# Adding the gates of three heads into a cleared DRAM map with indirect accumulating DMAs from GpSimd

## What is computed

```python
def peer_ffn(h, w_query, q_norm_peer, sub_keys_1, sub_keys_2, expert_u, expert_v):
    qr = rms_norm((h @ w_query).reshape(bsz, seq, PEER_HEADS, PEER_DKEY), q_norm_peer)
    ...
    v1, i1 = lax.top_k(s1, PEER_TOPK)
    v2, i2 = lax.top_k(s2, PEER_TOPK)
    ...
    top_s, top_pos = lax.top_k(cand_s, PEER_TOPK)
    idx = jnp.take_along_axis(cand_i, top_pos, axis=-1)
    g = jax.nn.softmax(top_s, axis=-1)
    ...
        act = jax.nn.gelu(jnp.einsum('td,ted->te', hx, u, preferred_element_type=jnp.float32))
        return jnp.einsum('te,ted->td', (gx * act).astype(vv.dtype), vv)
```

## Time and profile before

| | us |
|---|---|
| median of the runs | 2183.76 |
| span of the profiled execution | 2181.1 |
| runs' median less that span | 2.7 |
| TensorE busy | 2151.9 |
| VectorE busy | 1680.4 |
| ScalarE busy | 1233.9 |
| GpSimd busy | 245.7 |
| q1, the DMA queue of SP: packets' share of the 16 engines | 58.2% |

### The profile page before, as it was taken

One profiled execution on the slowest core, in us unless ns is written; L12 is line 12 of the kernel. 1 busy time (PEld: TensorE's weight loads), 2 busy tenths in 40 slices (PEclk: granted clock), 3 DMA queues, 4 the chain that ended last, 5 costly groups with the idle time before them and its releaser, 6 DMA issues.

```text
span 2181.1 us, 43026 instructions
## 1 busy us (share of the span) xinstructions
PE 2151.9 (99%) x15008; PEld 1989.8 (91%) x15008; DVE 1680.4 (77%) x3258; ACT 1233.9 (57%) x2168; POOL 245.7 (11%) x298
## 2 busy tenths in 40 slices
PE   6999999999999999999999999999999999999999
PEld 5889999999999988888888899999999999888887
DVE  8777777889499956777577878788886997567765
ACT  5656575444577655555566565644455776555554
POOL 0210000000166400000002100000002662000000
PEclk8999999999999999999999999999999999999999
DMA  9466655555533367787665666455555334687864
GB/s 352 156 223 229 204 188 173 182 182 182 184 122 110 125 193 260 258 253 231 192 202 176 221 231 206 162 183 183 179 177 175 115 116 144 200 272 258 254 211 171
DMA packets 115440, 427.29 MB, mean 196 GB/s; under 512 B 12816, under 2 KB 13072, under 8 KB 113680
## 3 DMA queue, kind: packets, MB, share of 16 engines
q1 hardware_dynamic: 115344, 426.08, 58.2%
HBM read 424.99 MB, written 1.05 MB: 195 GB/s over the span
## 4 chain that ended last, share of the span: by engine, by line
PE 96%; DVE 2%; ACT 1%; DMA 1%; issue 0%; SPq 0%; ACTq 0%; DVEq 0%
PE pj L1453 18%; PE pj L1455 18%; PE pj L1454 18%; PE wk L1453 11%; PE wk L1455 11%; PE wk L1454 11%; PE wk L1814 5%; PE wk L1583 1%; PE wk L1560 1%; DMA arena<-in_front 1%; PE wk L1576 1%; PE wk L1522 1%; DVE arena L878 0%; PE wk L1743 0%; ACT hi L496 0%
## 5 line engine op out<-in xcount | busy, mean ns | idle before, releaser
L873 DVE TENSOR_TENSOR lo<-raw,hi 128x1024 fp32r<-128x1024 f32 x683 | 843.3, 1236 | 417.7 <-ACT hi L496 412.1
L496 ACT ACTIVATE hi<-raw 128x1024 fp32r<-128x1024 f32 x683 | 721.4, 1057 | 470.9 <-PE wk L1455 341.5
L1453 PE MATMUL pj<-mov_hi,hi 128*128 128x256 f32 x3008 | 867.8, 288 | 1.8 <-DVE x L1204 1.3
L1455 PE MATMUL pj<-mov_hi,lo 128*128 128x256 f32 x3008 | 851.5, 283 | 0.0
L1454 PE MATMUL pj<-mov_lo,hi 128*128 128x256 f32 x3008 | 850.9, 283 | 0.0
L1453 PEld LDWEIGHTS pj<-mov_hi,hi 128*128 128x128 f32 x3008 | 577.0, 192 | 10.9 <-issue 8.3
L1454 PEld LDWEIGHTS pj<-mov_lo,hi 128*128 128x128 f32 x3008 | 576.5, 192 | 0.1
L1455 PEld LDWEIGHTS pj<-mov_hi,lo 128*128 128x128 f32 x3008 | 575.9, 191 | 0.0
L1453 PE MATMUL wk<-hi,mov_hi 128*128 128x512 f32 x1024 | 398.5, 389 | 0.0
L1454 PE MATMUL wk<-lo,mov_hi 128*128 128x512 f32 x1024 | 398.4, 389 | 0.0
L1455 PE MATMUL wk<-hi,mov_lo 128*128 128x512 f32 x1024 | 398.4, 389 | 0.0
(11 more groups left out here) (207 smaller groups left out, 1896.1 us busy)
## 6 DMA issues: line engine op xcount, KB each, us to landing
raw<-in_stream SPq DMA_DIRECT2D x684, 512.0 KB, 3.4
arena<-in_ada SPq DMA_DIRECT2D x72, 512.0 KB, 4.8
onehot_a<-in_ada SPq DMA_DIRECT2D x24, 512.0 KB, 4.3
arena<-in_front SPq DMA_DIRECT2D x8, 1024.0 KB, 14.8
arena<-in_taba SPq DMA_DIRECT2D x2, 1536.0 KB, 8.7
arena<-in_keys SPq DMA_DIRECT2D x2, 1024.0 KB, 5.5
x<-in_xT SPq DMA_DIRECT2D x1, 1024.0 KB, 14.8
arena<-in_mix SPq DMA_DIRECT2D x2, 512.0 KB, 4.2
```

Source lines behind the costliest of these rows:

```text
L496: nc.scalar.activation(hi[j % SPLIT][:, :], raw[j % RAW][:, :], ACT.Copy).then_inc(hi_done, 1)
L873: nc.vector.tensor_tensor(lo[j % SPLIT][:, :], raw[j % RAW][:, :], hi[j % SPLIT][:, :].bitcast(f32), ALU.subtract).then_inc(lo_done, 1)
L1453: pe.matmul(out, w_h, m_h, start=first, stop=False)
L1455: return pe.matmul(out, w_l, m_h, start=False, stop=last)
```

## The change

`GpSimd` clears a piece of SBUF at the start (`arena[:, 124:128, :]`, zeros, 128 by 1024). In the dense stage of the first layer SP writes this piece 32 times, once after each of the refills j = 8 to 39, and so clears the first 32768 columns of a new DRAM map `grid` (128 rows of 33792 fp32 values). In each layer VectorE works out, after the gates are ready, for heads 0 to 2, for both halves of the frames and all 16 picks, the place i1 * 33792 + i2 * 256 + frame in the map (`cell`) and copies the gates (`cell_gate`). After its last one-hot group GpSimd issues 96 indirect DMAs a layer (3 heads, 2 halves, 16 picks). Each adds 128 gates, one from each partition, to 128 single places of 4 bytes in the map. From the second head on it waits, before each group of 16, until all earlier DMAs of that half have landed. SP waits at the end of the kernel for all of them. Nothing reads the map.

```diff
--- before.py
+++ after.py
@@ -103,10 +103,13 @@
...
 C_ID, C_ONE, C_IOTA, C_EPS, C_C, C_PICK = 0, 128, 256, 384, 385, 385 + KC
-NCONST = 385 + KC + HEADS
+C_TOK = 385 + KC + HEADS
+NCONST = C_TOK + 2
 
...
 NMIX = 1024
+PITCH = NKEYS * SEQ + 1024
+MAPPED = 3
 
...
@@ -142,6 +145,10 @@
...
         onehot_a = sb("onehot_a", [P, 8, NKEYS])
+        cell = sb("cell", [P, 2, MAPPED * 16], u32)
+        cell_gate = sb("cell_gate", [P, 2, MAPPED * 16])
+        grid = nc.dram_tensor("grid", (P, PITCH), f32, kind="Internal").ap()
+        cells = grid.rearrange("p (c o) -> (p c) o", o=1)
 
...
@@ -325,6 +332,10 @@
...
         s_copied = sem("s_copied")
+        grid_zero = sem("grid_zero")
+        grid_clear = sem("grid_clear")
+        cells_ready = sem("cells_ready")
+        cells_added = [sem("cells_added_0"), sem("cells_added_1")]
         g_arg = sem("g_arg")
...
@@ -390,6 +401,12 @@
...
                     refill(L0 + j, j)
+                    if l == 0 and 8 <= j < 40:
+                        if j == 8:
+                            wait_alone(sp, grid_zero, 1)
+                        at = (j - 8) * 1024
+                        sp.dma_start(grid[:, at:at + 1024], arena[:, 124:128, :].rearrange("p a b -> p (a b)"))\
+                            .then_inc(grid_clear, 16)
                     if j == AHEAD - 1:
...
@@ -443,10 +460,13 @@
...
             sp.wait_ge(stored, KC // 2 * 16)
+            for b in range(2):
+                sp.wait_ge(cells_added[b], DEPTH * MAPPED * TOPK * 16)
 
...
         def _(pool):
+            nc.gpsimd.memset(arena[:, 124:128, :], 0.0).then_inc(grid_zero, 1)
             for l in range(DEPTH):
...
@@ -484,6 +504,18 @@
...
                     e.then_inc(hot_b[0], 1)
+
+                wait_alone(pool, cells_ready, l + 1)
+                if l == 0:
+                    wait_alone(pool, grid_clear, 32 * 16)
+                for h in range(MAPPED):
+                    for b in range(2):
+                        if l + h:
+                            wait_alone(pool, cells_added[b], (l * MAPPED + h) * TOPK * 16)
+                        for k in range(TOPK):
+                            pool.indirect_dma_start(cells, bass.IndirectOffsetOnAxis(ap=cell[:, b, h * 16 + k:h * 16 + k + 1], axis=0),
+                                                    cell_gate[:, b, h * 16 + k:h * 16 + k + 1], None,
+                                                    compute_op=ALU.add).then_inc(cells_added[b], 16)
 
...
@@ -1336,6 +1368,17 @@
...
                                         ALU.mult).then_inc(route_ready, 1)
+                split_early(1)
+                if l:
+                    for b in range(2):
+                        dve.wait_ge(cells_added[b], l * MAPPED * TOPK * 16)
+                dve.wait_ge(route_ready, l + 1)
+                link(nc.vector.tensor_scalar(pos_f, idx_tok, float(SEQ), None, ALU.mult))
+                link(nc.vector.scalar_tensor_tensor(pos_f[:, 0, :], idx_tok[:, 0, :], float(PITCH), pos_f[:, 1, :],
+                                                    ALU.mult, ALU.add))
+                for b in range(2):
+                    nc.vector.tensor_scalar(cell[:, b, :], pos_f[:, 0, b * P:b * P + MAPPED * 16], const[:, C_TOK + b:C_TOK + b + 1], None, ALU.add)
+                nc.vector.tensor_copy(cell_gate[:, :, :], top_s.rearrange("p (b h) k -> p b (h k)", b=2)[:, :, 0:MAPPED * 16]).then_inc(cells_ready, 1)
                 split_early(ROUTE_AT - early[0])
...
@@ -1957,6 +2000,7 @@
...
     const[:, C_PICK:C_PICK + HEADS] = (r[:, None] % 32) == np.arange(HEADS)[None]
+    const[:, C_TOK:C_TOK + 2] = r[:, None] + P * np.arange(2)[None]
     const[:, C_C:C_C + KC] = i["c"][0].reshape(KC, P).T
...
             "xT": xT}
```

## The result

The changed kernel takes 2200.43 us, the median of 2 runs (2199.02 to 2201.84), against 2183.76: a ratio of 1.0076 (95%: 1.006 to 1.0093). The forecast was 2187 us with a range of 2181 to 2240, and "within 2%" at 0.77. The class and this range hold. The size does not: 16.7 us slower, where 3 were forecast, and outside the range of 2182 to 2196 us that the forecast had for itself. The profiled span is 2199.6 us, 18.5 more than before (the slower of the two runs was profiled), and it is these 18.5 that have to be found.

A forecast was written before the change was run, and what follows sets the result against it. The prediction took TensorE, busy 2151.9 of 2181.1 us, to bound the kernel. It added 2.5 + 0 + 0 + 0 and 0.5 us for last waits, then 2.7 us from span to median: 2187 us, range 2181 to 2240.

The forecast's parts named there:

- the queue rival: Dense stage: the clearing writes overfill the DMA queue and cost 20 instead of 2.5 us; 2204 us, chance 0.06.
- Term 1: Dense stage: clearing writes make `in_ada` loads late, so VectorE and some softmax steps are late; 2.5 us, bounds 0 to 20.
- Term 2: VectorE's five new operations: 2.0 us a layer, caught up two tiles later; 0 us, bounds 0 to 1.
- Term 3: GpSimd's issue of 96 indirect DMAs a layer, behind the one-hots: 2.1 us each, within its room; 0 us.
- The first rival: GpSimd is too slow from 4.2 us per DMA, making the squares and the end late; 2284 us, chance 0.08.
- Term 4: DMA engines in the down projection: additions take 50 ns per element, 38 us a layer, with 106 us free; 0 us.
- the second rival: Down projection: additions fill the DMA engines from 0.14 us per element, TensorE waits for `raw`; 2359 us, chance 0.07.
- The third rival: Down projection: GpSimd's issue blocks VectorE and its `lo`, deciding from 0.7 us per DMA; 2247 us, chance 0.07.

The follow-up runs named there:

- e4_clears_early: The changed kernel with its 32 clearing writes moved to every second of the first 64 refills of `u` (319 to 503 us): 2184.57 us, ratio 1.0004.

## Why the prediction came out as it did

**The class** held, and by the reasons given for it: nothing of the change removes work, and the five operations of VectorE and the DMA engines in the down projection had the slack that the rows showed; GpSimd's room was just used up. The range of 2181 to 2240 us held because it was stretched for the rivals: 2200.43 us lies above the 2182 to 2196 us that stood for the forecast itself (0.72). (The chances are off by 0.01: the forecast and the queue rival, both within 2%, make 0.78, not 0.77.)

**Term 1, the clearing writes, was mis-sized: 2.5 us forecast, 13.3 us alone and 14.8 us with the rest measured.** The mechanism was named rightly (`in_ada` late, VectorE waits, the softmax steps are what TensorE sees), three of its steps failed in size. "Each now also stands behind a write, so it lands 1.3 us later": it lands 3.2 us later. A write takes 1.7 us of share, not 1.3; the remaining 1.5 us I put down to the load sharing the engines with write and refills over its whole way, which is argued, not shown. "VectorE's waits for `in_ada` up to 235 us grow from 8.4 to some 12 to 16 us": 19.7. "Two or three of them late by about 1 us": TensorE waited three times, 4.2, 3.8 and 1.7 us, and the first of these came to it through GpSimd's scaling, a path that the sum didn't have. And one step was missing altogether: with each of the two long waits the granted clock went to half for 6.83 us, which cost the other 5.2 us. The upper bound of 20 us held, and with it the rival "the clearing writes overfill the queue" (2204 us, chance 0.06), which is within 4 us of what was measured. That nearness is in part luck, since 3.7 us of the measured loss are GpSimd's. Its reason was only half right: a share of 0.98 was expected and 0.93 found, but with 0.81 the loss is still two thirds (writes of half the size), with 0.80 a third (other steps), and with 0.81 at the place of e4_clears_early nothing. The weight that I gave this rival came from asking whether the engines are full; the right question was which loads travel beside the writes and how much slack they have.

**Term 2**, 0 us: right. The delay of `lo` is 14.8 us behind the dense stage of layer 0 and still 14.8 us at the last tile, so the new operations on VectorE cost the stream nothing in either layer.

**Term 3, GpSimd's issue: 0 us forecast, 3.7 us at the end.** That the issue takes 2.04 us, where 2.1 stood, is luck: the 2.1 was the landing of a store, taken as the price of a whole DMA, and that price is 3.84 us. What failed is the step "32 DMAs stand between two waits and landings can overlap": only one to four stand between two waits, at each of which GpSimd lets all of them land, and this wait, 1.8 us for each DMA, is a term that the sum did not have. In layer 1 3.84 us stood against a room of 3.80: with 14.8 us lost before, the span would have ended at 2181.1 + 14.8 = 2195.9, the last issue ends at 2197.8, and its landing adds 1.8 to 2199.6; SP waits 3.1 us for it. So small a margin is chance: in the run with `in_ada` first the same DMAs came every 3.68 us, with the additions alone every 3.72, with the early writes every 3.74, and nothing was lost at the end of any of these three profiled runs; with the extra reads it was 3.84 again, and 4 us were lost. What makes the pitch differ by 4%, no run shows. In layer 0 3.86 against 4.19 left 33 us until the squares. The bounds, 0.33 and 4.5, held the 3.84. "The last indirect DMA is issued near 2018 us" was wrong by 178 us. The first rival's mechanism is real: its sign at the end, a chain that ends in `grid`, came, and two runs show the rest of it (83.1 and 52.7 us of TensorE waiting for the squares). In layer 0 of the changed kernel it stopped 0.3 us per DMA short.

The Trainium skill, "DMA: Bandwidth & Descriptors", section "Anatomy of one DMA — SWDGE (gpsimd) path", was cited for a cost of about 2.0 us of which most is the landing. The runs agree in kind and not in size: an adding DMA lands 2.9 to 8.4 us after its issue (median 5.5 in the additions alone), and the issue itself is 1.55 us or more. So the additions were not over sooner.

**Term 4**, 0 us: right. q0 holds 3.0% of 2199.6 us, 66 us or 33 a layer, where 38 were taken (50 ns per element). This is far from the 106 us that were free, so the second rival is out.

**The third rival**, `lo` held up by the issue, is out: in the down projection a `lo` beside an issue takes 1225.5 ns in the changed kernel, one beside none 1225.3, and before it was 1225.6. The Trainium skill infers in "SBUF — State Buffer", section "Who interferes with whom", that making descriptors needs the write side of the ports that VectorE and GpSimd share, which a VectorE operation with two inputs leaves free. For VectorE the trace agrees, by these numbers. For GpSimd it does not: in the run with 512 bytes the 51 issues beside no VectorE operation took 1.55 to 1.57 us, and in the changed kernel all 82 issues over 2.3 us ran beside a `lo`.

## What to carry to other kernels

Price an added transfer by the load that travels beside it with the least slack, not by the share of the engines: the same 32 writes cost 13.3 us beside loads for which VectorE was already waiting, and nothing measurable beside a stream that is three tiles ahead. For a train of GpSimd's adding DMAs count the issue, 0.3 us between two, and a wait for all of them to land (3.2 to 3.9 us here) divided by how many go out between two waits; hold that against the room per DMA up to whoever is next on GpSimd. Add to every TensorE wait of about 4 us what the clock takes after it, here 2.6 us.

## What the runs showed of the hardware

- Between two waits GpSimd issues one adding indirect DMA of 128 elements with a ring of 512 bytes, one to four with 1024, five or six with 1536, and it goes on only when all have landed; the pitch was 5.0, 3.8 and 3.2 us. Plain writes (32 packets instead of 144) go out seven or nine at a time, every 1.8 us.
- GpSimd's issue takes 1.55 us beside no VectorE operation and up to 2.6 us beside operations with two inputs; VectorE's own do not get slower (`lo` 1225.5 ns beside an issue, 1225.3 without).
- 512 KB written took 1.7 us of the DMA engines' share, 512 KB read 1.4 us, and 256 KB written in the halved kernel (0.71 - 0.46) x 59 us over 14.6 writes = 1.0 us.
- The granted clock went from 2.4 to 1.2 GHz during waits of TensorE of 4.2 and 3.8 us, and came back after 6.83 us each time. Shorter waits went both ways: behind one of 1.9 us (other steps) it was at half for 3.41 us, behind one of 1.7 us (changed kernel) and one of 2.3 us (other steps) it stayed full.
